# Where the split weights lie within 128 bytes of an SBUF partition

## What is computed

```python
x = x + hybrid_mixer(rmsnorm(x, norm_mix), w_in, ..., w_br, w_out)      # DeltaNet + mLSTM + stick-breaking attention
x = x + memory_cross_attention(rmsnorm(x, norm_xa), rmsnorm(mem, norm_mem), xa_wq, xa_wkv, xa_wo, ...)
x = x + conv_glu_ffn(rmsnorm(x, norm_ffn), ffn_up, ffn_conv, ffn_down)  # (silu(g) * u) @ w_down
```

## Time and profile before

| | |
|---|---|
| runs | 2004.33, 2003.33, 2003.0 us; median 2003.33 |
| the profiled execution's span | 2001.0 us, 2.3 us under the median of the runs |
| TensorE (PE) | busy 1987.1 us, 99% |
| VectorE (DVE) | 1216.1 us, 61% |
| ScalarE (ACT) | 892.0 us, 45% |
| DMA | 382.65 MB, mean 191 GB/s |
| TensorE's granted clock | 0.9 or more of 2.4 GHz in each of the 40 slices, mean 1.000 |

### The profile page before, as it was taken

How to read it: one execution, slowest core, us unless ns; L and a number is a source line. 1 busy time by engine, 2 the same in 40 slices (tenths; PEclk the granted TensorE clock), 3 DMA queues, 4 the chain that set the end, 5 groups by cost and what they waited for, 6 DMA issues and landing times.

```text
span 2001.0 us, 34706 instructions
## 1 busy us (share of the span) xinstructions
PE 1987.1 (99%) x14790; PEld 1895.9 (95%) x14790; DVE 1216.1 (61%) x1352; ACT 892.0 (45%) x877; POOL 40.5 (2%) x62
## 2 busy tenths in 40 slices
PE   8999999999999999999999999999999999999999
PEld 8999999999999999999999999988888888888888
DVE  5677645445454476576655345777777777754444
ACT  5445334434364343455434344544444444433333
POOL 1000100000000000000000000000000000000000
PEclk9999999999999999999999999999999999999999
DMA  8766754665557766565564456665656565566664
GB/s 268 220 192 195 226 159 143 198 200 166 182 174 247 243 198 223 169 194 186 178 199 129 139 168 198 212 208 171 207 171 206 173 204 174 177 205 223 185 203 134
DMA packets 356637, 382.65 MB, mean 191 GB/s; under 512 B 8144, under 2 KB 351604, under 8 KB 355124
## 3 DMA queue, kind: packets, MB, share of 16 engines
q1 hardware_dynamic: 350947, 353.36, 55.9%
q0 software_dynamic: 5584, 27.70, 4.0%
HBM read 367.47 MB, written 13.58 MB: 190 GB/s over the span
## 4 chain that ended last, share of the span: by engine, by line
PE 97%; DVE 1%; ACT 1%; DMA 0%; issue 0%; SPq 0%; DVEq 0%; ACTq 0%
PE bank L1961 18%; PE bank L1962 18%; PE bank L1963 18%; PE bank L1998 16%; PE bank L2000 8%; PE bank L2473 8%; PE bank L2474 4%; PE bank L2381 1%; PE bank L2400 1%; PE bank L2158 1%; DVE w_lo_home L1131 1%; ACT w_hi_home L540 0%; PE bank L2204 0%; PE bank L2061 0%; PE bank L2152 0%; DMA ident<-in_shape_masks 0%
## 5 line engine op out<-in xcount | busy, mean ns | idle before, releaser
L1131 DVE TENSOR_TENSOR w_lo_home<-raw,w_hi_home 128x2048 fp32r<-128x2048 f32 (+1 forms) x349 | 756.7, 2168 | 606.2 <-ACT w_hi_home L540 605.8
L540 ACT ACTIVATE w_hi_home<-raw 128x2048 fp32r<-128x2048 f32 (+2 forms) x359 | 645.0, 1798 | 1047.5 <-PE bank L1963 624.3
L1961 PE MATMUL bank<-x_home,w_hi_home 128*128 128x256 f32 x2304 | 648.1, 281 | 1.9 <-DVE w_lo_home L1131 1.9
L1962 PE MATMUL bank<-x_home,w_hi_home 128*128 128x256 f32 x2304 | 643.1, 279 | 0.0
L1963 PE MATMUL bank<-x_home,w_lo_home 128*128 128x256 f32 x2304 | 642.8, 279 | 0.0
L1998 PE MATMUL bank<-x_home,w_hi_home 128*128 128x512 f32 x1408 | 488.5, 390 | 0.1
L1961 PEld LDWEIGHTS bank<-x_home,w_hi_home 128*128 128x128 f32 x2304 | 433.1, 188 | 2.8 <-DVE w_lo_home L1131 1.4
L1962 PEld LDWEIGHTS bank<-x_home,w_hi_home 128*128 128x128 f32 x2304 | 433.2, 188 | 0.2
L1963 PEld LDWEIGHTS bank<-x_home,w_lo_home 128*128 128x128 f32 x2304 | 433.0, 188 | 0.0
L2000 PE MATMUL bank<-x_home,w_lo_home 128*128 128x256 f32 x1408 | 397.0, 282 | 0.0
L1998 PEld LDWEIGHTS bank<-x_home,w_hi_home 128*128 128x128 f32 x1408 | 264.2, 188 | 55.7 <-issue 0.4
(11 more groups left out here) (315 smaller groups left out, 1942.4 us busy)
## 6 DMA issues: line engine op xcount, KB each, us to landing
raw<-in_w_in SPq DMA_DIRECT2D x52, 2048.0 KB, 8.4
raw<-in_ffn_up SPq DMA_DIRECT2D x44, 2048.0 KB, 8.0
raw<-in_ffn_down SPq DMA_DIRECT2D x32, 1408.0 KB, 6.6
raw<-in_xa_wkv SPq DMA_DIRECT2D x16, 2048.0 KB, 9.3
raw<-in_w_br SPq DMA_DIRECT2D x8, 2048.0 KB, 8.4
raw<-in_w_out SPq DMA_DIRECT2D x8, 2048.0 KB, 8.3
raw<-in_xa_wq SPq DMA_DIRECT2D x8, 2048.0 KB, 8.3
raw<-in_xa_wo SPq DMA_DIRECT2D x8, 2048.0 KB, 8.4
```

Source lines behind the costliest of these rows:

```text
L540: return nc.scalar.activation(out_, in_, func, **kw)
L1131: tt(split_out(w_lo, kind, half), halves(raw, kind, half, par), split_out(w_hi, kind, half).bitcast(f32), ALU.subtract).then_inc(lo_ready, 1)
L1961: mm(o, w[0], x[0], start=start, stop=False)
L1962: mm(o, w[0], x[1], start=False, stop=False)
```

## The change

Nothing is added, removed or put in another order: on every engine the program has the same instructions with the same shapes in the same sequence. What changes is the element at which the split weights start within their half of `w_hi_home` and `w_lo_home`, for those who write and those who read them. In bytes past a multiple of 128:

| stage | weights before | weights after | d after (moving less stationary, modulo 128) |
|---|---|---|---|
| feature-major | 0 | 96 | 64 |
| UP, even and odd slot | 0 | 96, 112 | 64, 48 |
| DN, weight group 0, 1, 2, 3 | 0 | 32, 48, 64, 80 | 0, 112, 96, 80 |
| BV, CV (weights move) | 64 | 96 | 64 |
| V, unit 0 to 7 (weights move) | 64 | 96, 112, 0, 16, 32, 48, 80, 64 | 64, 80, 96, 112, 0, 16, 48, 32 |

```diff
 GDN_TAPS, FFN_TAPS = 4, 3
 EPS = 1e-6
 BIG = 1e30
+W_AT = 24
+UP_AT, DOWN_AT, V_AT = (24, 28), (8, 12, 16, 20), (24, 28, 0, 4, 8, 12, 20, 16)
+
+
+def place_of(name, i, par):
+    return {"UP": lambda: UP_AT[par], "DN": lambda: DOWN_AT[i], "V": lambda: V_AT[i]}.get(name, lambda: W_AT)()
+
 
 
 C_A = 0
@@ -131,8 +138,8 @@
         raw = sb("raw", [P, 2, KC * CW])
         w_hi_home = sb("w_hi_home", [P, 2, KC * P + 64], f32r)
         w_lo_home = sb("w_lo_home", [P, 2, KC * P + 64], f32r)
-        w_hi, w_lo = w_hi_home[:, :, 0:KC * P], w_lo_home[:, :, 0:KC * P]
-        wt_hi, wt_lo = w_hi_home[:, :, 16:16 + KC * P], w_lo_home[:, :, 16:16 + KC * P]
+        w_hi, w_lo = (t[:, :, W_AT:W_AT + KC * P] for t in (w_hi_home, w_lo_home))
+        home = lambda tile: w_hi_home if tile is w_hi else w_lo_home
         e_scope = ExitStack()
         x_back = sb("x_back", [P, KC, SEQ], f32, e_scope)
         o_tm = sb("o_tm", [P, TT, D], f32, e_scope)
@@ -394,11 +401,11 @@
             k = DG if kind == DOWN else KC
             return tile[:, slot, 0:k * CW].rearrange("p (k n) -> p k n", n=CW)[:, :, half * P:(half + 1) * P]
 
-        def split_out(tile, kind, half):
+        def split_out(tile, kind, half, at=W_AT):
             if kind == TM_:
-                return (wt_hi if tile is w_hi else wt_lo)[:, half, :]
+                return home(tile)[:, half, at:at + KC * P]
             k = DG if kind == DOWN else KC
-            return tile[:, half, 0:k * P].rearrange("p (k n) -> p k n", n=P)
+            return home(tile)[:, half, at:at + k * P].rearrange("p (k n) -> p k n", n=P)
 
 
         @block.gpsimd
@@ -544,7 +551,7 @@
                 act.wait_ge(raw_full[par], hp * 16 + 16)
                 if not (isinstance(hp, int) and 2 * hp + par == 0):
                     act.wait_ge(half_used, hp * 4 + (2 * par + half - 1))
-                copy(split_out(w_hi, kind_of[name], half), halves(raw, kind_of[name], half, par)).then_inc(hi_ready, 1)
+                copy(split_out(w_hi, kind_of[name], half, place_of(name, i, par)), halves(raw, kind_of[name], half, par)).then_inc(hi_ready, 1)
 
             def hi_part(part, name, i, par, hp, half):
 
@@ -553,7 +560,7 @@
                     if name != "A":
                         act.wait_ge(half_used, hp * 4 + (2 * par + half - 1))
                 ks = slice(part * (KC // 2), (part + 1) * (KC // 2))
-                copy(split_out(w_hi, FM, half)[:, ks, :], halves(raw, FM, half, par)[:, ks, :]).then_inc(hi_ready if part else wp_h, 1)
+                copy(split_out(w_hi, FM, half, place_of(name, i, par))[:, ks, :], halves(raw, FM, half, par)[:, ks, :]).then_inc(hi_ready if part else wp_h, 1)
 
             def hi(name, i, par, hp):
                 for half in range(2):
@@ -1128,15 +1135,17 @@
 
                 dve.wait_ge(hi_ready, hp * 4 + (2 * par + half + 1))
                 kind = kind_of[name]
-                tt(split_out(w_lo, kind, half), halves(raw, kind, half, par),
-                   split_out(w_hi, kind, half).bitcast(f32), ALU.subtract).then_inc(lo_ready, 1)
+                at = place_of(name, i, par)
+                tt(split_out(w_lo, kind, half, at), halves(raw, kind, half, par),
+                   split_out(w_hi, kind, half, at).bitcast(f32), ALU.subtract).then_inc(lo_ready, 1)
 
             def lo_part(part, n, name, i, par, hp, half):
 
                 dve.wait_ge(*((hi_ready, hp * 4 + (2 * par + half + 1)) if part else (wp_h, n)))
                 ks = slice(part * (KC // 2), (part + 1) * (KC // 2))
-                tt(split_out(w_lo, FM, half)[:, ks, :], halves(raw, FM, half, par)[:, ks, :],
-                   split_out(w_hi, FM, half)[:, ks, :].bitcast(f32), ALU.subtract).then_inc(lo_ready if part else wp_l, 1)
+                at = place_of(name, i, par)
+                tt(split_out(w_lo, FM, half, at)[:, ks, :], halves(raw, FM, half, par)[:, ks, :],
+                   split_out(w_hi, FM, half, at)[:, ks, :].bitcast(f32), ALU.subtract).then_inc(lo_ready if part else wp_l, 1)
 
             def lo(name, i, par, hp):
                 for half in range(2):
@@ -1983,7 +1992,8 @@
                 if kind == TM_:
                     for k in range(KC // 2):
                         kk = half * (KC // 2) + k
-                        w = [t[:, half, k * CW:(k + 1) * CW] for t in (wt_hi, wt_lo)]
+                        at = place_of(name, i, par) + k * CW
+                        w = [t[:, half, at:at + CW] for t in (w_hi_home, w_lo_home)]
                         for a in range(TT):
                             x = [acts[:, j, kk, a * P:(a + 1) * P] for j in range(2)]
                             last = three(bank[par + 2 * a][:, 0:CW], x, w, kk == 0, kk == KC - 1)
@@ -1995,9 +2005,10 @@
                         if ready and k % ready[2] == 0:
                             pe.wait_ge(ready[0], ready[1] + k // ready[2] + 1)
                         o = up_bank(par, half)
-                        mm(o[:, :].rearrange("p (j s) -> p j s", j=2), w_hi[:, half, k * P:(k + 1) * P], acts[:, :, k, :],
+                        at = place_of(name, i, par) + k * P
+                        mm(o[:, :].rearrange("p (j s) -> p j s", j=2), w_hi_home[:, half, at:at + P], acts[:, :, k, :],
                            start=k == 0, stop=False)
-                        last = mm(o[:, SEQ:2 * SEQ], w_lo[:, half, k * P:(k + 1) * P], acts[:, 0, k, :], start=False, stop=k == KC - 1)
+                        last = mm(o[:, SEQ:2 * SEQ], w_lo_home[:, half, at:at + P], acts[:, 0, k, :], start=False, stop=k == KC - 1)
                     for k in ks if name != "UP" else ():
                         if parts and k == KC // 2:
                             pe.wait_ge(lo_ready, whole)
@@ -2470,8 +2481,9 @@
                             if isinstance(c, int) and c == 0 and g * DG + k == FC - 2:
                                 pe.wait_ge(f_l, FC // 2)
                             o, x = bank[par + 2 * half], act_hl[:, :, g * DG + k, :]
-                            mm(o[:, :].rearrange("p (j s) -> p j s", j=2), w_hi[:, half, k * P:(k + 1) * P], x, start=g + k == 0, stop=False)
-                            last = mm(o[:, SEQ:2 * SEQ], w_lo[:, half, k * P:(k + 1) * P], x[:, 0, :], start=False,
+                            at = place_of("DN", g, g % 2) + k * P
+                            mm(o[:, :].rearrange("p (j s) -> p j s", j=2), w_hi_home[:, half, at:at + P], x, start=g + k == 0, stop=False)
+                            last = mm(o[:, SEQ:2 * SEQ], w_lo_home[:, half, at:at + P], x[:, 0, :], start=False,
                                       stop=g * DG + k == FC - 1)
                         last.then_inc(half_used, 1)
                     if g == 1 and not (isinstance(c, int) and c == 0):
```

## The result

The changed kernel takes 2006.89 us (median of 12 runs, 2004.3 to 2011.45) where the kernel before takes 2003.93 beside it (12 runs, 2003.0 to 2004.75): a ratio of 1.0020 [1.0012, 1.0027] (of the means; the medians are 0.15% apart). It is slower by 0.2%, little but clear of no change. The forecast of 1978.5 us, 1.25% faster, was wrong: the time lies inside the range of 1950 to 2044 us, but on the other side of no change. The changed kernel's runs spread over 7.2 us, those of the kernel before over 1.8. The profiled execution is one of the longer ones: span 2009.3 us, run 2011.45.

A forecast was written before the change was run, and what follows sets the result against it. TensorE's start-to-start distance was taken as the bound. Feature-major with BV and CV -19.6, UP -7.3, DN +1.9 and V +0.2 us sum to -24.8 on the 2001.0 us span; plus 2.3 gives 1978.5 us, range 1950 to 2044.

The forecast's parts named there:

- What bounds the kernel: TensorE, busy 99% of the span: time is the number of matmuls times the distance from start to start.
- let it shrink by the same factor for the next 32: Excess over the 110 ns floor falls from 10.0 to 6.7 ns by d = 32, again by two thirds to 64.
- fold d at 64: Distances priced symmetrically about d = 64: 96 like 32, 80 like 48, 112 like 16.
- The feature-major term: Feature-major stages with BV and CV, 8928 matmuls at d = 64, each 2.2 ns less: -19.6 us.
- the same factor on the pair's 20 ns: UP's 512 + 256 column pairs: 20 ns excess falls by 6.6 at d = 64, 3.7 at 48: -7.3 us.
- DN: +1.9 forecast: DN's 704 pairs, 176 a group, at +10, +4.5, 0 and -3.7 ns for d = 0, 112, 96, 80: +1.9 us.
- V: +0.2 forecast: V's 768 matmuls, 96 a unit over eight distances, gains and losses nearly cancelling: +0.2 us.
- No change: Rival: only d = 0 costs extra, all other distances are alike; 2004.8 us, chance 0.25.
- The pattern repeats every 64 bytes: Rival: d = 64 acts as d = 0, feature-major matmuls at 120.0 ns; +44.2 us, 2047.5 us, chance 0.21.
- The slower rhythm: Rival: d = 64 makes K's 353.5 ns a step, instead of 350, the rule; 2015.5 us, chance 0.10.
- To the floor: Rival: at d = 64 nothing is left of the excess over 110 ns; 88 us less, 1915 us, chance 0.04.
- the sum: Total of the feature-major, UP, DN and V terms: -24.8 us on the profiled span of 2001.0 us.

The follow-up runs named there:

- the kernel with only the front part moved: Against the kernel before, only the feature-major weights and BV and CV moved to 96 (d = 64), UP, DN and V as before: 1994.8 us, ratio 0.9966.
- the version with cuts: Kernel with only feature-major, BV and CV at d = 64, plus 24 matmul cuts of 32 + 224 columns where long streams start: 1985.84 us, ratio 0.9911.

## Why the prediction was wrong

- **What bounds the kernel: right.** TensorE's starts are the time, before and after; the splits (2291 and 1919 ns) and the waits did not move.
- **The step that failed: "I choose to let it shrink by the same factor for the next 32, and to fold d at 64", one price for each distance, from two points.** At d = 64 there are two paces. 113.3 ns is 1.2 ns better than the 114.5 forecast; 117.8 is 3.3 worse, and worse than the 116.7 before. In the changed kernel's trace 49 of the 176 halves of feature-major units hold the first, and all 10 of BV and CV; 126 hold the second, most of those in long stretches (GC, BR, most of WO, K, Q, XO). The feature-major term, with BV and CV, was forecast at -19.6 us and came to -2.8 in the profiled run (-1.2 and -1.6), one of the longest; in the median run it would be about -7 (an estimate: 3.0 us slower in all, less the 10.4 of UP, V and DN). BV and CV alone, in the fast rhythm throughout, gave -1.6 us where 480 x 2.2 ns = 1.1 was forecast. Had all held it, as the cuts show for most, the term would have been 8928 x -3.3 ns = -29.5 us.
- **UP: the same factor on the pair's 20 ns, -7.3 us forecast, +8.2 measured** (1408 x 5.8 ns). A pair at 64 and at 48 takes 352.6 and 352.4, the slow one of the two levels of pairs. This term alone is 15.5 us off, and it is most of the loss: without it, DN and V the front part is faster (ratio 0.9966). The factor was taken from threes, and no row of a pair at another distance stood behind it; both signs should have been priced there. At d = 32 UP already had 346.7, the least that a pair took at any place, so it had nothing to win.
- **DN: +1.9 forecast, about +1.2 measured, near it by luck.** Group 0 at d = 0 was to be the slowest at 356; it is at 347.7 in the mean, and group 2 at d = 96, forecast unchanged, is at 352.4. 176 x (1.0 + 0.1 + 5.7 + 0.2) ns = 1.2 us. The fold failed too: 96 is not like 32.
- **V: +0.2 forecast, +1.0 by the stages.** Unit 4 at 119.8 was right; unit 0 (d = 64) at 117.8 was not the fastest, and unit 1 (d = 80) went at 119.9 where 115.5 was forecast. No unit went under the 116.7 of the earlier trace rows.
- **The rivals.** "No change" named a time, 2004.8, within 2.1 us of the measured one, but not the reason: other distances are not alike. "The pattern repeats every 64 bytes" is refuted: d = 64 never reads 120. "The slower rhythm" had the mechanism: the earlier trace rows showed that a stream can hold another pace at one address. It lacked the faster of the two. It was given 0.10 because it is seldom seen at d = 32 (18 of 202 halves of threes in the trace before); that it is rare there said nothing on how often it holds elsewhere. "To the floor" is refuted: nothing goes under 113.3.
- **A rule of the Trainium skill** was weighed against the sum: "TensorE: Matmul & The Clock Gate", section "Step-by-step: what each phase is for", by which the load of the next weights takes no read bandwidth from the running matmul. From that the prediction drew that place would be nothing. The traces differ: 113.3 to 121.3 ns for one shape at a granted clock of 1.00, with nothing changed but places. The measurement decides; but the rule's time, no change, was nearer than the sum.

What stays open: what in the chip makes the two rhythms. In the changed kernel most streams that start with 205 to 207 ns between their first two matmuls go fast and those with 200 to 202 or 305 mostly go slow, with exceptions; that is a correlation, and which comes first was not tried. What picks the level of a stream of pairs is open as well. That the spread of the changed kernel's runs comes from a different share of fast stretches in each run fits the spread of the kernel with only the front part moved (6.9 us) and the narrow one of the version with cuts (2.0 us), but only one trace of each was seen. Fewer cuts, other widths at the same places, and cuts in pairs were not tried.

## What to carry to other kernels

Where back-to-back matmuls are the bound, read the distance from start to start by stage and over at least ten steps, and look whether a stage has one pace or two, before putting a price on it. Move one stage at a time: here the two halves of the change, -3 to -10 and +10 us, cancelled in the total. A state that depends on how a stream starts can be worth setting on purpose: 24 small cuts, 2.7 us of cost, turned a place that gave 0.3% into 0.9%.

## What the runs showed of the hardware that was not expected

- A stream of 128x256 float32r matmuls with a weight load each, at a granted clock of 1.00, takes 113.3 to 121.3 ns a matmul by where its operands start within 128 bytes of a partition.
- At d = 64 it holds 113.3 or 117.8 ns, the first through 18 us and three changes of half with no cut in one trace; a matmul cut into 64 + 192 or 32 + 224 columns can turn the one into the other, and a 512-column matmul turned it back (340 to 353.3 ns a step, without a pause).
- A pair of 512 and 256 columns has two levels of its own at places in steps of 16 bytes, 346.7 and about 353 ns. It held the lower at d = 32, 80 and 112, the upper at 48 and 64, and at 0, 16 and 96 one after the other; the best distance of the threes (64) is a slow one for pairs.
